# A streaming-encoder block on one core: weight tiles split into high and low parts, in halves or whole

## What is computed

```
h = modulate(rmsnorm(x), shift_a, scale_a)
proj = h @ w_in                      # 1024 x 4104
mixed = token_mix(proj)              # 4 retention heads, 4 gated DeltaNet heads, chunks of 64
x = x + gate_a * (mixed @ w_out)     # 1024 x 1024
h = modulate(rmsnorm(x), shift_m, scale_m)
x = x + gate_m * (square(relu(h @ w_ff1)) @ w_ff2)   # 1024 x 4096, 4096 x 1024
return rmsnorm(x)
```

## Time and profile before

| | |
|---|---|
| median of 3 runs | 2854.47 us (2853.68 to 2855.95) |
| the profiled execution | 2852.43 us |
| its span | 2850.6 us |
| TensorE's busy time | 2784.6 us |
| VectorE, ScalarE, GpSimd busy | 1380.4, 1094.1, 1670.8 us |
| mean granted TensorE clock | 0.996 of full speed |

### The profile page before, as it was taken

How to read it: one execution, slowest core, us unless ns; L and a number is a source line. 1 busy time by engine, 2 the same in 40 slices (tenths; PEclk the granted TensorE clock), 3 DMA queues, 4 the chain that set the end, 5 groups by cost and what they waited for, 6 DMA issues and landing times.

```text
span 2850.6 us, 37254 instructions
## 1 busy us (share of the span) xinstructions
PE 2784.6 (98%) x14080; PEld 2337.0 (82%) x14080; DVE 1380.4 (48%) x1982; ACT 1094.1 (38%) x1893; POOL 1670.8 (59%) x1260
## 2 busy tenths in 40 slices
PE   5999999999999999999999999999999999999998
PEld 4788888888888888888888888888888888888886
DVE  5756565464656555553445436553353443322233
ACT  3533343353334434343344433343333333443332
POOL 3755553676566656575555755676565556665653
PEclk9999999999999999999999999999999999999999
DMA  7333344332333324322233323422222224233242
GB/s 273 120 119 137 130 146 157 121 115 89 104 118 123 96 74 133 104 86 85 85 119 93 111 67 104 147 79 93 78 86 82 85 78 141 89 98 101 90 126 88
DMA packets 98098, 311.64 MB, mean 109 GB/s; under 512 B 11520, under 2 KB 11520, under 8 KB 95872
## 3 DMA queue, kind: packets, MB, share of 16 engines
q1 hardware_dynamic: 67248, 246.85, 27.2%
q10 hardware_dynamic: 30672, 62.40, 6.6%
HBM read 285.09 MB, written 24.12 MB: 108 GB/s over the span
## 4 chain that ended last, share of the span: by engine, by line
PE 85%; DVE 4%; POOL 2%; issue 2%; ACT 1%; DMA 1%; ACTq 0%; DVEq 0%; POOLq 0%
PE acc L491 24%; PE acc L493 24%; PE acc L492 23%; PE pm L527 8%; PE pm L532 2%; POOL mT L1645 1%; DVE mixing L1217 1%; PE pm L626 1%; PE pm L631 1%; PE pm L582 0%; ACT io L767 0%; PE pm L642 0%; PE pm L541 0%; PE pm L641 0%; PE pm L627 0%
## 5 line engine op out<-in xcount | busy, mean ns | idle before, releaser
L1636 POOL TENSOR_TENSOR w<-raw,w 128x512 fp32r<-128x512 f32 x832 | 1130.5, 1361 | 1015.7 <-ACT w L738 1014.3
L738 ACT ACTIVATE w<-raw 128x512 fp32r<-128x512 f32 x832 | 520.8, 627 | 780.2 <-PE acc L493 725.5
L491 PE MATMUL acc<-mT,w 128*128 128x512 f32 x1536 | 624.6, 407 | 6.1 <-DVE mT L1530 3.2
L493 PE MATMUL acc<-mT,w 128*128 128x512 f32 x1536 | 601.2, 391 | 0.0
L492 PE MATMUL acc<-mT,w 128*128 128x512 f32 x1536 | 599.6, 390 | 0.0
L491 PE MATMUL acc<-hid,w 128*128 128x512 f32 x864 | 351.7, 407 | 2.3 <-DVE ffs L1431 1.4
L491 PEld LDWEIGHTS acc<-mT,w 128*128 128x128 f32 x1536 | 289.8, 189 | 63.0 <-issue 4.8
L493 PEld LDWEIGHTS acc<-mT,w 128*128 128x128 f32 x1536 | 288.9, 188 | 62.9
L493 PE MATMUL acc<-hid,w 128*128 128x512 f32 x864 | 338.4, 392 | 0.0
L492 PE MATMUL acc<-hid,w 128*128 128x512 f32 x864 | 337.3, 390 | 0.0
L492 PEld LDWEIGHTS acc<-mT,w 128*128 128x128 f32 x1536 | 290.2, 189 | 53.1 <-issue 1.0
(11 more groups left out here) (223 smaller groups left out, 3661.9 us busy)
## 6 DMA issues: line engine op xcount, KB each, us to landing
raw<-in_w_all SPq DMA_DIRECT2D x416, 512.0 KB, 3.5
ada_late<-in_ada_w SPq DMA_DIRECT2D x32, 512.0 KB, 5.4
xr<-in_xT ACTq DMA_DIRECT2D x48, 256.0 KB, 3.4
mixing<-in_ada_w SPq DMA_DIRECT2D x8, 1024.0 KB, 10.0
proj_kept<-ffs ACTq DMA_DIRECT2D x32, 256.0 KB, 2.1
out<-io ACTq DMA_DIRECT2D x32, 256.0 KB, 2.4
mixed_kept<-mixing ACTq DMA_DIRECT2D x28, 256.0 KB, 2.2
xr<-mixed_kept ACTq DMA_DIRECT2D x28, 256.0 KB, 2.7
```

What stands on the lines that cost most here:

```text
L491: e.matmul(bank, whi, x[:, 0, :], start=first, stop=False)
L493: m = e.matmul(bank, wlo, x[:, 0, :], start=False, stop=last)
L738: e.activation(w2[:, 0, local % HALVES, :], raw[:, tile % NRAW, local % 2 * NT:(local % 2 + 1) * NT], ACT.Copy).then_inc(S["w_hi"], 1)
L1636: e.tensor_tensor(w2[:, 1, local % HALVES, :], raw[:, tile % NRAW, local % 2 * NT:(local % 2 + 1) * NT], w2[:, 0, local % HALVES, :].bitca ...
```

## The change

`hi` and `lo` do nothing for an even `local`. For an odd one they treat both halves of its tile in one instruction of 1024 columns, and raise their semaphore by 2. The calls stay where they are, so an instruction stands where that of the second half stood. The waits are those of the odd half.

```diff
             def hi(local):
+                if local % 2 == 0:
+                    return
                 tile = local // 2
                 e.wait_ge(RAWSEM[tile % NRAW], 16 * (tile // NRAW + 1))
                 if local >= HALVES:
                     e.wait_ge(S["w_used"], local - HALVES + 1)
-                e.activation(w2[:, 0, local % HALVES, :], raw[:, tile % NRAW, local % 2 * NT:(local % 2 + 1) * NT],
-                             ACT.Copy).then_inc(S["w_hi"], 1)
+                at = 2 * tile % HALVES
+                e.activation(w2[:, 0, at:at + 2, :].rearrange("p a c -> p (a c)"), raw[:, tile % NRAW, :],
+                             ACT.Copy).then_inc(S["w_hi"], 2)
...
             def lo(local):
+                if local % 2 == 0:
+                    return
                 tile = local // 2
                 e.wait_ge(S["w_hi"], local + 1)
-                e.tensor_tensor(w2[:, 1, local % HALVES, :], raw[:, tile % NRAW, local % 2 * NT:(local % 2 + 1) * NT],
-                                w2[:, 0, local % HALVES, :].bitcast(F32), ALU.subtract).then_inc(S["w_lo"], 1)
+                at = 2 * tile % HALVES
+                e.tensor_tensor(w2[:, 1, at:at + 2, :].rearrange("p a c -> p (a c)"), raw[:, tile % NRAW, :],
+                                w2[:, 0, at:at + 2, :].rearrange("p a c -> p (a c)").bitcast(F32),
+                                ALU.subtract).then_inc(S["w_lo"], 2)
```

## The result

The changed kernel takes 2905.41 us (median of 4 runs, 2899.17 to 2907.17), the kernel before 2854.61 (4 runs, 2853.68 to 2855.95). The ratio is 1.0175, with a 95% interval from 1.0163 to 1.0187: 1.75% slower, 50.8 us. I had forecast 2886, 33 us more, with a range of 2860 to 2912. The direction and the mechanism were right, the size was two thirds of what came. (My own sum, 33 us on the median before, gives 2887 and not 2886.)

What follows compares the result with a forecast made beforehand. TensorE, busy 98% of the span, was taken to bound the kernel. Stalls of 29.9 us, less 3 given back, plus 6 for VectorE behind GpSimd made +33, so 2886 us, with an 8 in 10 range of 2860 to 2912.

Steps and rivals of the forecast that it cites:

- Durations: Whole-tile splits of 1024 columns: 1.06 us on ScalarE, 2.45 us on GpSimd; busy time down some 80 and 55 us.
- the rival that the width isn't taken: An engine works 1024 columns at the price of two halves: +5 us, within the forecast's own range; no separate chance.
- Where TensorE would wait: At a tile's first matmul, for GpSimd's split: some 20 to 30 waits, 29.9 us in the sum.
- two reloads: Reload of the residual, twice: ScalarE reaches its order late behind VectorE's wait for a transfer; stalls of 5.7 and 5.5 us.
- first window, two tiles: ScalarE's late order makes two tiles late by 3.4 and 3.3 us, mostly the same delay; 3.8 us for both.
- lesser ones: Some twelve smaller TensorE stalls of 0.1 to 1.5 us each, 7.5 us together.
- What a stall gives back: New stalls shorten TensorE's later waits for VectorE's L1287 (six, 7.5 us); 3 us given back.
- VectorE behind GpSimd: In the recurrence, VectorE stands still behind longer GpSimd instructions: 16 hits of 0.4 us, 6 us, bounds 0 and 16.
- Loads: ScalarE's waits for raw tiles, 18 times and 31.3 us, become fewer; worth 0, bounds 0 and 4.0 us.
- The buffers absorb it: Rival: over 380 of 416 tiles have slack, so time is unchanged, 2850 to 2858 us; chance 0.08.
- faster: Rival: fewer instructions relieve ScalarE and GpSimd, ending TensorE's 11.2 us of waits for L1287 and L1365: 2841 us; chance 0.05.
- Late on every tile: Rival: slower splits make some 90 more tiles lose 0.4 us each, 2922 us; chance 0.07.

Runs made afterwards that it cites:

- the place alone: Against the kernel before: both halves of a tile ordered at the second half's place, each still its own instruction on ScalarE and GpSimd; 2874.66 us, ratio 1.0071.
- experiment on readiness or blocking: Against the kernel with ScalarE whole and GpSimd in halves: TensorE is told of both low halves only after the second; 2896.53 us, ratio 1.0142 to the kernel before.
- held kernel: Against the kernel before: GpSimd makes the low part of four single halves 6, 8, 10 and 14 times more; 2882.01 us, ratio 1.0099.
- order-first kernel: Against the changed kernel: at output projection tiles ScalarE makes the next tile's high part ahead of the square waiting for VectorE; 2896.99 us, ratio 1.0148.

## Why the prediction was right, and where it was short

- **Durations.** Right. ScalarE's 1024 columns take 1054 ns (I took 1058), GpSimd's 2456 (2450). The estimate of 2.25 us from the Trainium skill (GPSIMD Engine Reference, section 3.1) is reached by none of the 416: the shortest, as at the reload, takes 2.34 us. Both are below the price of two halves (2 x 627 and 2 x 1290 ns), so the rival that the width isn't taken falls. GpSimd's busy time fell by 97.6 us and not 55, since I had compared with two undisturbed halves, and the old mean of 1361 ns held the stretching by VectorE.
- **Where TensorE would wait.** Right in kind: 16 waits, not 20 to 30, of 37.5 us, for a sum of 29.9.

  | place | predicted, us | measured, us |
  |---|---|---|
  | two reloads | 5.7 + 5.5 | 8.4 + 7.5 |
  | first block's second normalisation | 4.8 | 4.3 |
  | first window, two tiles | 3.8 | 3.0 + 2.6 |
  | last block's normalisation | 2.6 | 2.6 |
  | lesser ones | 7.5 (some twelve) | 9.2 (ten) |

  At the reloads the time from ScalarE's order to TensorE's start came out as put (3.58 us for 3.59 and 0.25); it was the order that was later. The first reload is issued 0.8 us before the tile's start and not 1.9, and took 2 us longer to land. The first window in the end cost nothing: at 200 us TensorE is 1.8 us ahead of the kernel before.
- **What a stall gives back.** I put 3 us; the waits for L1287 fell by 7.0 (7.5 to 0.5), of which 5.7 behind new stalls. That made up for half of the 7.6 us that the last point lacked.
- **VectorE behind GpSimd.** I put 6 us in the recurrence. L1328, L1359 and L1365 and their successors went from 1.2 + 1.4 + 3.7 = 6.3 to 12.2 us, 5.9 more. That this is the number I put is luck: with the place alone and no wide instruction they are already 10.0 us, and only 3 to 4 us separate the kernels with GpSimd in halves and ScalarE whole (8.9 and 8.1) from the change. Wide instructions do hold VectorE: its busy time grew by 48.1 us, and by 3.3 with the place alone. The experiment on readiness or blocking gives it about 8.9 us of the total, clock and all.
- **Together** these terms made +33, and TensorE's idle time grew by 35.4. The agreement to 3 us is in part luck: the waits were 7.6 us more than put and what the stalls gave back 4.0 more.
- **The step that failed** is the unspoken one, that TensorE's busy time stays at 2784.6. It grew by 16.6 us. The clock was 0.996 before, the kernel had almost no waits after the start, and I read a share that was near 1 as a constant. It isn't one: behind the waits of 8.4 and 7.5 us at the reloads TensorE ran at half its clock, and lost 2.5 and 2.9 us more in the two halves behind, of which 1.3 came back each time on the next. A term of 2 to 3 us for each of the longest stalls, as the held kernel shows it too, belonged in the sum. With the stalls at the normalisations it makes about half of the 16.6 us; 2.1 us may be chance, and where the rest comes from wasn't followed up.
- **Loads.** Right: ScalarE's 31.3 us of waits for raw tiles in the earlier trace rows are no longer among its waits; the order comes half a tile later than the load now needs.
- **The rivals.** "The buffers absorb it" and "faster" fall with 37.5 us of new waits. "Late on every tile" falls with their number, 16. That TensorE stands behind few late orders, and not behind all tiles, is what the order-first kernel shows directly: it moves one instruction ahead of one wait, and about half of the loss at the two reloads goes.

The rule that speaks against the change (the Trainium skill, Perfetto Trace Analysis, Optimizing Scalar/DVE Operations: break instructions up where ScalarE or VectorE, not saturated themselves, cause bubbles on other engines) is the one that the runs bear out. ScalarE at 38% and GpSimd at 59% had time to spare, but TensorE had none to lose. The rule doesn't speak of GpSimd; here GpSimd's width cost 24 us, and ScalarE's 6.6 (with GpSimd in halves) or nothing (with GpSimd whole).

## What to carry to other kernels

Here 176 us of busy time saved on two engines that weren't the bound bought nothing; what counted was how long before its use the work was ordered, less how long it took until it was signalled. Write down for a buffered operand: lead minus latency, here 8.16 - 2.0 us before and 5.44 - 3.6 after, and look for the places where a producer's order stands behind an unrelated wait longer than that. This tells where a stall comes, not how much it costs in all: the kernel with two halves of lead had a margin of 3.2 us by it and lost 31. Then price each large stall of a matmul engine that was always busy with its length and the lower clock behind it, 2 to 3 us here.

## What the runs showed that I had not expected

- **A stall's price has a second part.** TensorE's granted clock fell behind long waits: 0.74 in the 20 us around the first reload, where the kernel before had 1.00. In the kernel with held low parts, stalls of 1.8 and 3.5 us cost nothing more, 5.9 and 11.0 us cost 2.6 and 2.0 us more. The length of the wait alone doesn't decide it: after a wait of 1.8 us the clock fell in the order-first kernel and not in the change.
- **Lost clock can move.** In the order-first kernel it came back in part at the reloads and went at 1245 and 1950 us, 1.6 us each.
- **Moving one order moved a part of the stall.** In the same kernel the 8.4 us became 0.9 and, one tile later, 3.5 us; the whole brought 8.4 us of time, where 17 were expected.
- **One wide GpSimd instruction holds VectorE longer than two narrow ones**, though it moves the same data in less time: 1428.5 us of VectorE's busy time against 1372.1, and about 8.9 us of the kernel's time.
- **Half the lead was worth more than I thought.** The kernel before lost 31 us with its halves ordered two ahead and not three, although by my sum each half still had 3.2 us to spare.
